# Two-block transformer forward on one core: the first mixer's compressed branch, its projections and the modulation vectors in another order

## The reference

```python
def adaln_norm(x, c, g, w_ada, b_ada):
    mod = silu(c) @ w_ada + b_ada                 # 1024 x 3072
    shift, scale, gate = split(mod, 3)
    h = rms_norm(x, g) * (1 + scale) + shift
    return h, gate

def nsa_mixer(h, ...):                            # 16 heads of 64 in 2 groups
    q, k_c, v_c, k_s, v_s, k_w, v_w, z, g_logit = split(h @ w_in)
    def compress(a, pe, w1, w2):                  # 15 blocks of 32 tokens, stride 16
        return silu((blocks(a) + pe) @ w1) @ w2   # hidden rows: 30 (2 groups x 15) x 256
    k_cmp, v_cmp = compress(k_c, ...), compress(v_c, ...)
    o_cmp = softmax(mask(q @ k_cmp)) @ v_cmp
    o_slc = selected-block attention(rope(q), rope(k_s), v_s)
    o_win = window attention(rope(q), rope(k_w), v_w)
    o = gates[0] * o_cmp + gates[1] * o_slc + gates[2] * o_win
    return (o * silu(z)) @ w_out
```

## Time and profile before

| | |
|---|---|
| median of 3 runs | 1289.66 us (1282.10, 1289.66, 1290.29) |
| profiled execution | 1284.67 us; its span 1282.8 us |
| busy share of the span | PE 91%, DVE 67%, ACT 43%, POOL 13% |
| mean granted clock | 0.958 |
| DMA | 221.61 MB, mean 173 GB/s; the SP queue of the ring 51.6% of 16 engines |

### The profile page before, as it was taken

One profiled execution on the slowest core, in us unless ns is written; L12 is line 12 of the kernel. 1 busy time (PEld: TensorE's weight loads), 2 busy tenths in 40 slices (PEclk: granted clock), 3 DMA queues, 4 the chain that ended last, 5 costly groups with the idle time before them and its releaser, 6 DMA issues. The chain is left out here.

```text
span 1282.8 us, 19888 instructions
## 1 busy us (share of the span) xinstructions
PE 1165.7 (91%) x7647; PEld 963.4 (75%) x7647; DVE 864.1 (67%) x1454; ACT 551.3 (43%) x987; POOL 161.1 (13%) x113
## 2 busy tenths in 40 slices
PE   4878798989999889999989998898988898999997
PEld 4665577867778678887868885797888776888786
DVE  4784599579978659955569965895465647455554
ACT  1232256352356543444457763434232336444432
POOL 0011134012141200000100001100404011000011
PEclk9989799899999899999999999898898899999999
DMA  7878155348854459965635553793000044655462
GB/s 257 290 251 264 49 181 167 114 127 282 295 187 158 125 158 317 327 207 181 195 107 192 165 177 115 248 344 121 4 2 3 18 148 149 197 191 167 168 190 73
DMA packets 143480, 221.61 MB, mean 173 GB/s; under 512 B 10823, under 2 KB 66715, under 8 KB 143259
## 3 DMA queue, kind: packets, MB, share of 16 engines
q1 hardware_dynamic: 140512, 216.37, 51.6%
q10 hardware_dynamic: 2875, 3.98, 0.9%
HBM read 219.27 MB, written 1.05 MB: 172 GB/s over the span
## 5 line engine op out<-in xcount | busy, mean ns | idle before, releaser
L535 PE MATMUL bank<-w_parts,lhs_hi 128*128 128x512 f32 (+2 forms) x960 | 391.0, 408 | 12.8 <-ACT w_parts L489 6.9
L489 ACT CAST w_parts<-ring 128x1024 fp32r<-128x1024 f32 (+2 forms) x288 | 289.6, 1033 | 256.8 <-PE bank L537 59.0
L494 DVE TENSOR_TENSOR w_parts<-ring,w_parts 128x1024 fp32r<-128x1024 f32 (+2 forms) x272 | 337.6, 1276 | 81.0 <-ACT w_parts L489 80.0
L537 PE MATMUL bank<-w_parts,lhs_lo 128*128 128x512 f32 (+2 forms) x960 | 383.5, 400 | 0.0
L550 PE MATMUL bank<-w_parts,lhs_hi 128*128 128x512 f32 (+2 forms) x960 | 271.9, 398 | 11.1 <-DVE w_parts L494 11.0
L535 PEld LDWEIGHTS bank<-w_parts,lhs_hi 128*128 128x128 f32 x960 | 186.4, 194 | 53.6 <-issue 14.0
L550 PEld LDWEIGHTS bank<-w_parts,lhs_hi 128*128 128x128 f32 x960 | 179.8, 190 | 53.9 <-DVE w_parts L494 16.8
L537 PEld LDWEIGHTS bank<-w_parts,lhs_lo 128*128 128x128 f32 x960 | 185.9, 194 | 36.7
L665 DVE SCALAR_TENSOR_TENSOR ada_acc<-ring,c_act,ada_acc 128x512 f32<-128x512 f32 x203 | 165.5, 815 | 13.4 <-DMA ring<-in_ada_w 3.0
L535 PE MATMUL bank<-w_parts,up_hi 128*128 128x512 f32 x176 | 69.2, 393 | 0.0
L826 POOL TENSOR_TENSOR x<-x,xn 128x512 f32<-128x512 f32 x10 | 17.7, 1788 | 409.0 <-DVE xn L817 409.0
...
## 6 DMA issues: line engine op xcount, KB each, us to landing
...
```

The costliest lines, as they stand in the source:

```text
L489: eng.copy(hi, raw).then_inc(hi_ready, 1)
L494: eng.tensor_tensor(lo, raw, hi.bitcast(F32), ALU.subtract).then_inc(lo_ready[who], 1)
L535: pe.matmul(b, x_hi, w, start=(k0 + k == 0), stop=False)
L537: mm = pe.matmul(b, x_lo, w, start=False, stop=False)
```

## The change

The output nsa 4 is taken out of the attention: its products are laid into the compressed branch, 24 behind the scores, 8 behind the turn of the probabilities, 8 behind each half of the weighted sums. The attention has nsa 5 only, 28 of its 48 products; POOL splits only nsa 5. The hidden rows of the compressed branch are computed turned: weights stationary (128 columns), block rows moving (30), 64 matmuls in all for k and v, not 32; ACT's silu writes hidT and the "hid" turn falls away. kc and vc are turned in the middle of nsa 0, ks and kw in nsa 1 behind its first 12 products; the first hidden rows stand between nsa 0 and nsa 1. Vectors: ada 5 comes behind nsa 0's weights and its sum in nsa 1; ada 6 and 7 behind nsa 4's weights, 8 and 9 with nsa 5; of their 32 steps 12 lie in the compressed branch (CMP_ADA) and 20 in the attention; ada 10 to 13 in halves behind dil 1 to 5; 14 and 15 beside the dilated attention; 16 to 23 behind eight outputs of ffn1, 24 to 27 behind z and the first two gates, 28 and 29 in ffn2. Sums 6 to 9 and 12 to 15 write four separate columns each of bank 7 and are collected together (TOGETHER); the others of the hybrid mixer are summed one output later.

```diff
+FFN_ADAS = {"ffn1": {j: 15 + j for j in range(1, 9)}, "ffn2": {1: 28, 2: 29}}
+TOGETHER = {n: range(a, a + 4) for a in (6, 12) for n in range(a, a + 4)}
...
-BESIDE = (("nsa", 4), ("nsa", 5), ("dil", 6), ("dil", 7))
+BESIDE = (("nsa", 5), ("dil", 6), ("dil", 7))
+Z_OUT = {"nsa": (4, 5), "dil": (6, 7)}
...
+CMP_ADA = (4, 4, 4)
...
-    s += [gemm("nsa", 2, w, 1024, 512, both), ada(4), kw_gates, ada(5)]
-    s += [gemm("nsa", 0, w, 0, 512, both), ada(6), gemm("nsa", 1, w, 512, 512, both), ada(7)]
-    s += [("pe", ("cmp", 0), column_units([(ck, 0, 256)], 256, 16, 2 * CHUNKS), None),
-          ("pe", ("cmp", 1), column_units([(cv, 0, 256)], 256, 16, 2 * CHUNKS), None)]
-    s.append(beside([(("nsa", 4 + j), w, 1792 + 512 * j) for j in range(2)], range(8, 12), 2))
+    first_cmp, second_cmp = [("pe", ("cmp", i), column_units([(c, 0, 256)], 256, 16, 2 * CHUNKS), None)
+                             for i, c in enumerate((ck, cv))]
+    s += [gemm("nsa", 2, w, 1024, 512, both), ada(4), kw_gates]
+    s += [gemm("nsa", 0, w, 0, 512, both), ada(5), first_cmp]
+    s += [gemm("nsa", 1, w, 512, 512, both), second_cmp]
+    s += [gemm("nsa", 4, w, 1792, 512, act), ada(6), ada(7)]
+    s.append(beside([(("nsa", 5), w, 2304)], range(8, 10), 2))
     s += [gemm("nsa_out", j, o, 512 * j, 512, gated) for j in range(2)]
-    for j in range(6):
-        s.append(gemm("dil", j, dw, 512 * j, 512, dve if j < 4 else act))
-        if j:
-            s.append(ada(11 + j))
-    s.append(beside([(("dil", 6 + j), dw, 512 * (6 + j)) for j in range(2)], range(17, 19), 1))
+    lots = {n: iter(ada(n)[2]) for n in range(10, 14)}
+
+    def mixed(keys, freers):
+
+        (stage, j), *small = keys
+        units = column_units([(dw, 512 * j, 512)], 512, KC)
+        return ("beside", [(stage, j)] * len(units) + [("ada", n) for n in small],
+                units + [next(lots[n]) for n in small], freers)
+
+    behind = ((), (10, 10), (10, 10), (11, 11), (11, 11, 12, 12), (12, 12, 13, 13, 13, 13))
+    parts = [mixed([("dil", j), *behind[j]], dve if j < 4 else act) for j in range(6)]
+    s.append(("beside_more", [key for part in parts for key in part[1]], [u for part in parts for u in part[2]],
+              {("dil", j): parts[j][3] for j in range(6)}))
+    s.append(beside([(("dil", 6 + j), dw, 512 * (6 + j)) for j in range(2)], range(14, 16), 1))
...
-        s += [gemm("gate", j, w, BA_AT + GATE_W * (j + 1), GATE_W, act), ada(26 + j)]
+        s += [gemm("gate", j, w, BA_AT + GATE_W * (j + 1), GATE_W, act)]
+        if j < 2:
+            s.append(ada(26 + j))
...
+        def sum_columns(n):
+            if n in TOGETHER:
+                return bank[7][:, 4 * (n % 6):4 * (n % 6) + 4]
+            return bank[n] if n < SUMS else bank[7]
...
+                pe.wait_ge(mod_ready, TOGETHER[n][0] if n in TOGETHER else n)
...
-            stream_end["dve"] = plan.outputs["ada", 7][1][-1]
+            stream_to("dve", plan.outputs["nsa", 1][1][2])
+            read_turns("dve", "ks", lambda b: ksT.rearrange("p g t -> p (g t)"), [0])
+            stream_to("dve", plan.outputs["nsa", 1][1][3])
+            ada_collect_up_to(6)
+            stream_end["dve"] = plan.outputs["nsa", 1][1][-1]
             rope_parts(dve, ("nsa", 1), lambda tt: gemm_bank("nsa", 1, tt)[:, :], 8)
             stream_end["dve"] = None
-            ada_collect_up_to(8)
-
-            await_turn(dve, "hid")
-            hb = turn_bank("hid")[:, 0:4 * G * NCMP].rearrange("p (v c m) -> p v c m", v=2, c=2)
-            dve.tensor_copy(hidT, hb)
+
+            ada_done = [0]
+
+            def some_ada(n):
+                for _ in range(n):
+                    ada_beside(6, ada_done[0])
+                    ada_done[0] += 1
+
+            dve.wait_ge(hidden_act, 2)
             for c in range(2):
-                src = hb[:, 1, c, :].rearrange("p (g n) -> p g n", g=G)
+                src = hidT[:, 1, c, :].rearrange("p (g n) -> p g n", g=G)
                 for g in range(G):
                     ins = dve.tensor_copy(hid_rep[:, c, g, :, :], src[:, g:g + 1, :].broadcast_to([P, HG, NCMP]))
-            ins.then_inc(turn_read["dve"], 1)
+            ins.then_inc(hidden_spread, 1)
+            read_turns("dve", "qp", lambda b: qpT[:, 2 * b:2 * b + 2, :].rearrange("p c t -> p (c t)"), range(4))
+            stream_to("dve", plan.outputs["nsa", 4][1][1])
...
+            stream_to("dve", plan.outputs["nsa", 4][1][3])
+            some_ada(CMP_ADA[0])
...
+            some_ada(CMP_ADA[1])
...
+            some_ada(CMP_ADA[2])
...
+            n_before = ada_done[0]
+
+            def ada_in_attention(i):
+                some_ada(n_before + (32 - n_before) * (i + 1) // 32 - ada_done[0])
+
+            nsa_att.dve(dve, link, weigh, ada_in_attention, lambda: None, first_half)
...
+            def hidden_rows(kv):
+                act.wait_ge(pe_units, plan.units[plan.outputs["cmp", kv][1][-1]][2] + 1)
+                for c in range(2):
+                    ins = act.activation(hidT[:, kv, c, :], bank[6 + c][:, kv * G * NCMP:(kv + 1) * G * NCMP], ACT.Silu)
+                ins.then_inc(hidden_act, 1)
+
...
+                if j == 0:
+                    hidden_rows(0)
+                    stream_to("act", plan.outputs["nsa", 1][1][2])
+                    read_turns("act", "kw", lambda b: kwT.rearrange("p g t -> p (g t)"), [0])
...
-            nsa_att.act(act, lambda p: beside_act(act, "nsa", p // 2 + 1, p == 9, z_act))
+            take_beside(act, "nsa", 4, z_act)
+            nsa_att.act(act, lambda p: beside_act(act, "nsa", p // 5, False, z_act))
...
-                stream_to("pool", units[min(grp + 2, len(units) - 1)])
+                stream_to("pool", units[grp // 2])
...
-            project(2)
-            ada_sum(pe, 4)
-            project(3, 304)
-            ada_sum(pe, 5)
-
...
-            project(0)
-            ada_sum(pe, 6)
-            project(1)
-            ada_sum(pe, 7)
...
-                        mm = pe.matmul(bank[6 + kv][0:G * NCMP, 0:CMP_HIDDEN],
-                                       blocks[:, kv, j, :, :].rearrange("p g n -> p (g n)"),
-                                       ring[:, unit % RING, k * 256:(k + 1) * 256], start=(j == 0), stop=(j == 15))
+                    for c in range(2):
+                        for k in range(2 * CHUNKS):
+                            j = 2 * CHUNKS * u + k
+                            at = k * CMP_HIDDEN + c * P
+                            mm = pe.matmul(bank[6 + c][:, kv * n:(kv + 1) * n], ring[:, unit % RING, at:at + P],
+                                           blocks[:, kv, j, :, :].rearrange("p g n -> p (g n)"),
+                                           start=(j == 0), stop=(j == 15))
                     mm.then_inc(pe_units, 1)
+
+            def some(steps, n):
+                for _ in range(n):
+                    next(steps)
+
+            project(2)
+            project(3, 304)
+            ada_sum(pe, 4)
+            o2 = plan.outputs["nsa", 2][0]
+            for tt in range(TT):
+                pe.wait_ge(bank_free["dve", tt], plan.free_count("dve", tt, o2))
+            steps = gemm_steps(pe, "nsa", 0, from_lhs, "norm0", 512)
+            some(steps, 24)
+            turn_keys("kc", kc2)
+            turn_keys("vc", vc2)
+            some(steps, 24)
+            hidden_rows(0)
+            steps = gemm_steps(pe, "nsa", 1, from_lhs, "norm0", 512)
+            some(steps, 12)
+            pe.wait_ge(rope_done, 2)
+            turn_keys("ks", ks2)
+            pe.wait_ge(rope_done, 4)
+            turn_keys("kw", kw2)
+            some(steps, 24)
+            pe.wait_ge(hidden_act, 1)
+            ada_sum(pe, 5)
+            for _ in steps:
+                pass
+            hidden_rows(1)
...
             mm.then_inc(cmp_scored, 1)
+            steps = gemm_steps(pe, "nsa", 4, from_lhs, "norm0", 512)
+            some(steps, 24)
             pe.wait_ge(cmp_exp, 1)
             turn(pe, "pc", 0, [(p_cmp[:, tt, HG * g:HG * g + HG, :].rearrange("p h n -> p (h n)"), P, HG * NCMP,
                                 (2 * tt + g) * P) for tt in range(TT) for g in range(G)])
+            some(steps, 8)
             await_turns_read(pe, "pc", [0])
             for i in range(4):
...
+                if i % 2:
+                    some(steps, 8)
...
-            products = beside_products(pe, "nsa", (4, 5), "norm0", 6)
-            nsa_att.pe(pe, products, 102 - BEHIND)
+            products = beside_products(pe, "nsa", (5,), "norm0", 0)
+            nsa_att.pe(pe, products, 48 - BEHIND)
...
-            for n in range(8, 12):
+            for n in range(6, 10):
                 ada_sum(pe, n)
...
-                    ada_sum(pe, 11 + j)
+                if j in (3, 5):
+                    ada_sum(pe, 10 if j == 3 else 11)
...
+            for n in range(12, 16):
+                ada_sum(pe, n)
             into_norm(pe, 1, from_lhs, "dil_o")
...
-                if j < len(adas):
```

(13 more changed lines are left out.)

147 lines of the change are left out of this document (70 added, 77 removed).

## The result

The changed kernel takes 1277.5 us in the median of 16 runs (1267.0 to 1284.4), the kernel before 1287.9 (16 runs, 1282.1 to 1291.9): ratio 0.9914, interval 0.9895 to 0.9934. It gains 11 us where 32 were forecast. The profiled execution of the changed kernel, 1284.24 us, is one of its longest, and that of before, 1284.67, one of the shorter; so the two traces end within 1 us of each other and the difference of the medians is not in them: between these two profiles 31 us of the forecast gain are missing, by the medians 21. A difference that only one profile of the changed kernel shows is not called the change's. Two that agree can still mislead: the experiments leave many stages as the change made them, and their profiles say how far a stage moves by itself.

What follows compares the result with a forecast made beforehand. PE bounds the first feed-forward, DVE the attention and dilated projections, a chain of short steps the compressed branch. Terms -8 -9 -7.2 -8.3 +3.3 -1.5 -4.5 +3.6 give -31.6: 1284.67 to 1253 us (median 1258), range 1240 to 1275.

Steps and rivals of the forecast that it cites:

- A: Projections and compressed branch up to the attention: -8 us, bounds -11 and -2; attention begins at 144.1, not 153.75.
- Its own bound: Turned hidden products of the compressed branch: some 0.4 us each at the lower clock, the branch's upper bound, +12 us.
- Rival 4: Slower: clock from 62 to 144 us falls at hand-overs; gain gone from mean 0.69 down, 1302 us at 0.62; chance 0.05.
- Rival 5: Compressed branch: nsa 4's products find no waits, loaded DVE ends as late; start +1, total -22, 1267 us; chance 0.06.
- B: Attention: -9 us, bounds -13 and -3; 7.2 us per pair of steps, 55 us from first to last scores.
- The new wait: Attention start: first product waits for ACT's cast behind two exponentials, so step 1 starts at +5.3 us, not +2.5.
- C: Sums behind the attention: four small ones in a row take 3.3 us, not 10.5, gaining -7.2 us.
- D: Dilated projections: half vectors free DVE, dilated attention starts near 354, not 362.5; -8.3 us, bounds -10 and -4.
- The sums behind the dilated attention: Four small sums now stand behind the dilated attention, costing +3.3 us.
- E: Later stages: first feed-forward -1.5 us (bound +5), gates -4.5 (bounds -8 and -2), second feed-forward +3.6.
- rival 3: DMA limit in feed-forward and gates: repeats with vectors run late, leaving -8 us, 1281 us; chance 0.07.
- Gates: Hybrid mixer gates: vector 26's sum one product group later, fewer vectors and gate sums; -4.5 us, bounds -8 and -2.

Runs made afterwards that it cites:

- again: The changed kernel with nothing altered, run for a second profile: 1278.5 us, 0.9915 of the kernel before.
- rows_alone: The kernel before with only the turned hidden rows, no hid turn or its copies, ACT reading the first group before the second: 1300.3 us, 1.0105.
- gates_collect: The changed kernel with DVE collecting vector 26's sum behind the low parts of gate 2, not gate 3: 1272.2 us, 0.9881 of the kernel before.
- ada_sooner: Changed kernel with old-shape hidden rows and cast, sums and gates edits, plus 16 vector steps in branch and 16 in attention, not 12 and 20: 1261.2 us.
- ada_later: Changed kernel with old-shape hidden rows and cast, sums and gates edits, plus 8 vector steps in branch and 24 in attention, not 12 and 20: 1258.2 us.
- sums_apart: The changed kernel with sums 6 to 9 and 12 to 15 each behind 7 wide products, not in a row: 1274.2 us, 0.990 of the kernel before.

## Why the prediction was wrong

It named the right places. It left the clock that narrow products cost out of its terms, and overlooked one order of work on DVE. By its steps, from the profiles after and again:

- **A, forecast -8, measured +0.3 and -0.4** (-2.6, -3.8 and -2.9 in the three experiments with the same branch). The step that failed: "so 0.22 each, 14.1 us for 64: no gain and no loss". The groups took 19.3 us, 17.4 to 20.0 in the five profiles, and 26.8 when put alone into the kernel before (rows_alone). Its own bound, 0.4 us each at the lower clock, was the right price for a good part of them. That nsa 4's products would be covered was right: PE waits for DVE and ACT only 3.3 us in 88. But then every narrow group of the branch is on the path with its clock. Rival 4 named the clock, but for hand-overs between short groups, where it fell inside long narrow ones with no pause; it put the end of the gain at 0.69; the mean of the stretch is 0.84, and 14 us of 88 are clock. It was priced as a catastrophe and not as a term. Rival 5 has the right number for A (+1) by another mechanism, a branch that ends when DVE does; PE, not DVE, is busy to its end.
- **B, forecast -9, measured -4.6 and -4.5** (and nothing in gates_collect, where the clock fell at the end). The new wait was foreseen and is larger by 1.1 (6.4 for 5.3 to the second scores, part of it half clock). The pace is 7.6 us a pair for 7.2: the second half of the term was mis-sized, and the 7.5 that the forecast had worked out for DVE, and then went below, was nearer. That DVE alone sets the pace is not so (ada_sooner and ada_later).
- **C, forecast -7.2, measured -6.4** for the sums, and 1.3 given back by the clock behind them: -5.1. **D, forecast -8.3, measured -6.2** from the product behind the sums to the dilated scores, or -7.5 without that 1.3. Vectors no longer end PE's waits. **The sums behind the dilated attention, forecast +3.3:** they are 3.6 long and lose another 3.6 to half clock behind (12.9 for 9.3). The term lacked the clock. From the last dilated scores to the row scales it is 46.7 us for 39.1, and moving the sums brings back 1 of these 7.6. Another 1.3 to 3.7 are lost at the first dilated steps, at half clock in every profile behind the change but that of sums_apart (33.3 us before from the first to the last dilated scores, 36.6 and 34.6 after); no run shows what brings that fall.
- **E.** First feed-forward, forecast -1.5, measured -1.4 (434.9 to 589.8 and 429.6 to 583.2). Its eight repeats with a vector take 12.5 us, or 13.4 with a gate's sum, none late: rival 3 did not come. Behind it, up to z 0, a gain of 1.5 that the forecast did not have. Second, forecast +3.6, measured +3.4 (but +0.5 to +0.8 in four of the experiments). **Gates, forecast -4.5, measured +0.8 and +1.1:** the step that failed is that vector 26's sum "stands one product group later" and so is covered. What counts is when DVE collects the sum before it, and the change put that behind low parts which need weights that PE uses last in gate 2. gates_collect turns it into -4.2 against before, the forecast's size.
- **Recurrence, forecast nothing, measured +3.1 and +2.8.** No edit touches it, yet it takes 142.7 us before, 145.8 and 145.5 after, and 140.5 to 145.7 in the other variants; the gates' stretch, too, is 92.7 to 96.6 in variants that don't touch it. What one is shorter the other is longer: both together are 234.9 us before (235.5 in rows_alone), 238.3 to 238.9 in all seven profiles with the changed gates, and 228.5 in gates_collect. So of the gates and the recurrence +3.9 is the change's, where -4.5 was forecast. The recurrence's chain has waits of 4.8 us and half clock at places that shift with the time at which it begins; why its length changes is not shown.

Added up against the forecast for the profile again: A 7.7, B 4.5, C and D 2.5, the dilated attention and its sums 5.6, gates and recurrence 8.4, less 1.5 behind the first feed-forward and 0.1 in the two feed-forwards together: 27 us, the 31.6 forecast less the 4.5 between its span and the span before. By the medians 21 are missing; how these 21 divide is not known, since the profiles of the stages differ by as much as 4 us.
